# Three column tiles (32, 32 and 64 wide) in place of two of 64 in the expert products of a transformer block

## What is computed

```python
hg = jnp.einsum('nd,edf->nef', tk, we_gate).astype(jnp.float32)
hu = jnp.einsum('nd,edf->nef', tk, we_up).astype(jnp.float32)
act = (jax.nn.silu(hg) * hu * gk[..., None]).astype(tk.dtype)
return jnp.einsum('nef,efd->nd', act, we_down).astype(jnp.float32)
```

## Time and profile before

| what | value |
|---|---|
| median of 2 runs | 1309.55 us (1309.27 to 1309.84) |
| span of the profiled execution | 1309.2 us |
| its own time | not listed apart; the two runs lie 0.1 and 0.6 us above its span |
| expert loop (first to last matmul of L1188) | 632.5 to 1247.0 us |
| PE busy | 1257.5 us, 96% |
| mean granted TensorE clock | 0.986 of full speed |

### The profile page before, as it was taken

The page is one execution under the profiler, slowest core; times in us unless marked ns, Lnnn a source line. Parts: engine busy times, 40 slices in busy tenths (PEclk is TensorE's granted clock), DMA queues, the critical chain, the costliest instruction groups (busy, mean ns, idle before and its releaser), DMA issues.

```text
span 1309.2 us, 22611 instructions
## 1 busy us (share of the span) xinstructions
PE 1257.5 (96%) x6217; PEld 714.6 (55%) x6217; DVE 837.3 (64%) x1769; ACT 737.0 (56%) x964; POOL 191.5 (15%) x373
## 2 busy tenths in 40 slices
PE   2999999999999999989999999999999999999996
PEld 2778788876777788875433333333333333333332
DVE  6746778567787655797556555555565555555578
ACT  3356462334544422212477777777777777777711
POOL 1000000000100100131122222122212221222100
PEclk9799999998999999998999999999999999999999
DMA  8722446659843370545779999999999999998395
GB/s 322 245 65 96 154 138 223 225 188 231 224 162 66 118 268 33 185 163 207 276 309 376 344 401 407 388 383 407 403 352 406 381 404 392 397 403 331 108 389 235
DMA packets 111458, 353.67 MB, mean 270 GB/s; under 512 B 20502, under 2 KB 59527, under 8 KB 85810
## 3 DMA queue, kind: packets, MB, share of 16 engines
q1 hardware_dynamic: 92498, 303.05, 62.5%
q0 software_dynamic: 18912, 50.01, 10.5%
HBM read 326.08 MB, written 47.21 MB: 285 GB/s over the span
## 4 chain that ended last, share of the span: by engine, by line
PE 83%; DVE 11%; DMA 2%; issue 2%; ACT 1%; POOL 0%; SPq 0%; DVEq 0%; ACTq 0%; POOLq 0%
PE bank L1188 27%; PE bank L1213 13%; PE bank L882 10%; PE bank L884 9%; PE bank L883 9%; PE bank L1175 4%; PE bank L1198 2%; PE bank L951 2%; PE bank L1077 2%; PE bank L975 1%; DVE acc_first L1653 1%; DMA y_all<-y_rows 1%; DVE x L2310 1%; PE bank L962 1%; DMA x_rows<-u_rows,row_index 1%
## 5 line engine op out<-in xcount | busy, mean ns | idle before, releaser
L1188 PE MATMUL bank<-gu_use,x_t 128*64 128x512 f32 x1664 | 368.5, 595 | 0.0
L1526 ACT ACTIVATE gu_use<-gu 128x1024 f32 x208 | 209.0, 1058 | 51.8 <-PE bank L1188 36.5
L1188 PEld LDWEIGHTS bank<-gu_use,x_t 128*64 128x64 f32 x1664 | 114.9, 137 | 216.4 <-issue 216.2
L1519 ACT ACTIVATE down_use<-down 128x2048 f32 x103 | 190.9, 1900 | 0.0
L1213 PE MATMUL bank<-down_use,act_t 128*64 128x512 f32 x832 | 187.4, 592 | 0.0
L882 PE MATMUL bank<-h_hi,w_lo 128*128 128x512 f32 x448 | 182.9, 408 | 2.3 <-DVE w_lo L1670 1.3
L884 PE MATMUL bank<-h_hi,w_hi 128*128 128x512 f32 x448 | 176.7, 394 | 0.0
L883 PE MATMUL bank<-h_lo,w_hi 128*128 128x512 f32 x448 | 176.6, 394 | 0.0
L2184 DVE COPY gu_use<-gu 128x1024 f32 x208 | 133.0, 690 | 53.7 <-PE bank L1188 33.3
L1670 DVE TENSOR_TENSOR w_lo<-stream,w_hi 128x1024 fp32r<-128x1024 f32 x72 | 87.9, 1221 | 98.3 <-ACT w_hi L1303 98.2
L2150 DVE TENSOR_TENSOR pick<-slot_id,places 128x512 bf16<-128x512 f32 x53 | 36.7, 692 | 145.5 <-POOL columns L797 145.5
(11 more groups left out here) (323 smaller groups left out, 1664.7 us busy)
## 6 DMA issues: line engine op xcount, KB each, us to landing
gu<-in_we_gate SPq DMA_DIRECT2D x64, 1024.0 KB
gu<-in_we_up SPq DMA_DIRECT2D x64, 1024.0 KB, 8.8
down<-in_we_down SPq DMA_DIRECT2D x64, 1024.0 KB, 8.7
stream<-in_w_in SPq DMA_DIRECT2D x28, 1024.0 KB, 7.1
ada_w<-in_w_ada POOLq DMA_DIRECT2D x8, 2048.0 KB, 9.7
y_rows<-zeros SPq DMA_DIRECT2D x8, 2048.0 KB, 14.7
y_all<-y_rows SPq DMA_DIRECT2D x8, 2048.0 KB, 14.9
ada_first<-in_w_ada SPq DMA_DIRECT2D x16, 512.0 KB, 10.4
```

The lines of the kernel that those rows point to most:

```text
L1188: last = nc.tensor.matmul(bank[item.par][rows, :], x_t[:, k, rows], gu_use[h][:, :, k, :], start=(k == 0), stop=(k == KD - 1))
L1519: nc.scalar.activation(down_use[h][:, :, :], down[:, bass.ds(slot, 1), :, :].rearrange("p o k n -> p (o k) n"), ACT.Copy).then_inc(down_ta ...
L1526: return nc.scalar.activation(gu_use[h][:, 1, ks, :], gu[:, bass.ds(slot, 1), 1, ks, :].rearrange("p o k n -> p (o k) n"), ACT.Copy)
```

## The change

`BY_COLUMNS` names three column tiles: slots 0 to 31 and 32 to 63, both with the weights of half 0, and slots 64 to 127 with those of half 1. Both products loop over these three in place of the two halves. What is computed, the operands in memory, the PSUM banks, the semaphores and their counts are as before. For each block there are three matmuls in place of two, two of them 32 columns wide, and these two stream the same moving operand.

```diff
 HP = P // 2
+BY_COLUMNS = ((0, slice(0, HP // 2)), (0, slice(HP // 2, HP)), (1, slice(HP, P)))
 MIN_PAIRS = T * TOPK // (4 * HP)
...
                     for k in range(part * KD // 2, (part + 1) * KD // 2):
-                        for h in range(2):
-                            rows = slice(h * HP, (h + 1) * HP)
+                        for h, rows in BY_COLUMNS:
                             last = nc.tensor.matmul(bank[item.par][rows, :], x_t[:, k, rows], gu_use[h][:, :, k, :],
                                                     start=(k == 0), stop=(k == KD - 1))
                     last.then_inc(gu_half, 1)
...
                     for f in range(FE):
-                        for h in range(2):
-                            rows = slice(h * HP, (h + 1) * HP)
+                        for h, rows in BY_COLUMNS:
                             last = nc.tensor.matmul(bank[5 + half][rows, :], act_t[:, f, rows], down_use[h][:, f, cols],
                                                     start=(f == 0), stop=(f == FE - 1))
                 last.then_inc(y_done, 1)
```

## The result

| what | before | after |
|---|---|---|
| median of 2 runs | 1309.55 us | 2002.1 us (2001.81 to 2002.39) |
| ratio, 95% interval | | 1.5281 (1.5248 to 1.5313) |
| span of the profiled execution | 1309.2 us | 2000.1 us |
| mean granted clock | 0.986 | 0.994 |

The forecast was 2000 us. The kernel is slower by half, and all of the loss is in the expert loop. In the changed kernel the lines before `gate_up` lie one further down, the down product is L1212, and the code behind it one line up.

The account below looks back on a forecast made before the run. TensorE was taken to bound the expert loop: 10.30 us of streaming and 2.98 us of shape changes, 13.28 us an item, times 52 = 690 us on 1309.2 us, giving 2000 us; range 1845 to 2204 us.

Parts of the forecast that it names:

- TensorE sets the end of the loop: Expert loop, 11.90 us an item: whatever is added to TensorE's stream is added to the time, 52 times.
- A change of the tile's shape empties the array, whether or not the columns meet: Each block of both products: narrow tiles stream, array empties, 64-wide tile streams alone, array empties again; serial case 0.80.
- Rival (a): Blocks of L1188 and L1213: all three tiles stream together, no added streaming, 1310 us; chance 0.14.
- rival (b): Blocks of both products: two streams at a time, third tile waits without emptying, 268 us more, 1577 us; chance 0.03.
- Streaming: 12 x 0.858 us an item: Twelve blocks an item in gate_up and project_down: 1.716 us each in place of 0.858, adding 10.30 us an item.
- The changes: 0.14 into 64 and 0.12 into 32: Changes of tile width, twelve each way an item, less one 0.14 already there: 2.98 us an item.
- The rest of the kernel stays: Outside TensorE's added loop time: what lies beside it costs nothing, and all before 632 us is unchanged.
- Rival (c): Loop: serial case with granted clock falling to 1.2 GHz, every streaming pass doubles, about 3070 us; chance 0.03.

Follow-up runs that it names:

- Experiment 4: Changed kernel with only two tiles, 32 columns at 0 and 64 at 64, slots 32 to 63 left out: 1997.04 us; kernel before 1311.67 us.
- experiment 1: Changed kernel with four tiles of 32 columns in both products: 1312.83 us, ratio 0.9997 to the kernel before.
- experiment 6: Changed kernel with three tiles of 32 columns at 0, 32 and 64, slots 96 to 127 left out: 1309.13 us; kernel before 1310.79 us.
- experiment 5: Changed kernel with two tiles, 48 columns at 0 and 64 at 64, slots 48 to 63 left out: 1309.98 us; kernel before 1310.79 us.
- Experiment 3: Changed kernel with the same 32, 32 and 64 tiles grouped by width, 8 width changes an item, not 24: 1892.28 us, ratio 1.441 to the kernel before.
- experiment 2: Changed kernel with even blocks as two tiles of 64, odd blocks as four of 32: 1390.66 us, ratio 1.059 to the kernel before.
- experiment 7: Changed kernel with 32, 32 and 64 in gate and up only, down product in two tiles of 64: 1768.54 us, ratio 1.347 to the kernel before.

## Why the prediction was right

- *TensorE sets the end of the loop.* Right: the loss is TensorE's own terms, item by item, while DVE and ACT did the same work as before and the DMA engines fell to 0.46 of their time. Whether DMA, at 0.93 before, would have held the loop if TensorE had been any faster was not tried.
- *A change of the tile's shape empties the array, whether or not the columns meet.* This was the step on which everything hung, and the rows of before could not decide it: in each of them the new tile covered columns in use, and a rule by which only such a tile waits would have given the same gaps. The prediction said so and chose, at 0.80; that the choice held is in part luck. Experiment 4 shows it for columns that never meet, experiments 1 and 6 that neither the number of tiles nor the shared operand matters, and experiment 5 sharpens it: the class counts, not the number of columns. Rival (a), three together, falls by the result itself, and rival (b), two at a time, by experiments 1, 4 and 6. "Emptying" is the name for what the rows show: nothing of the other class is loaded or started until the streaming has ended and 0.10 us more have passed. What goes on in the array meanwhile no row shows.
- *Streaming: 12 x 0.858 us an item.* Right. Experiment 3 takes most changes of width away and leaves this term nearly alone: an item of it is 11.22 us over the 11.90 of before, where 10.30 of streaming and 0.89 of changes were expected.
- *The changes: 0.14 into 64 and 0.12 into 32.* Slightly small. Twelve blocks of 1.985 in place of 0.858 are 13.5 us, less the change of 0.14 that stood before gate_up already: 13.37 us an item measured (25.27 less 11.90), 13.28 forecast. What was left out is the stagger of the second narrow tile, 0.007 a block, which is hidden while the width stays and open at each change (experiments 2 and 4 fit this). It is 12 x 0.007 x 52 = 4.4 us.
- *The rest of the kernel stays.* Nearly. It came out shorter, which hid most of the loop's excess: luck, if of 0.2% only. From the first gate_up to the end of the last down product the profiled executions took 1951.32 - 630.72 = 1320.6 us against 1258.37 - 632.54 = 625.8: 694.8 us more, where 690 were forecast. The stretch before the loop was 1.8 us shorter in this execution, and the tail 2.0 us shorter (2000.1 - 1951.32 against 1309.2 - 1258.37). The span grew 690.9 us in sum. No experiment was made on this, but the two traces show where it lies. Ahead of the loop, the lower clock level fell on other stretches. From 296 to 303 us the kernel before was granted 0.51 of the clock, and the same matmuls (L883 at 297.33 to L951 at 303.23) took it 5.90 us; the kernel after, at 1.00 there, took 3.28 us for them (L884 at 298.24 to L952 at 301.52). Other such stretches give part of these 2.6 us back. In the tail, PE of the kernel before waited 0.99 us for a DMA (the first line below), with the DMA engines at 1.00 of their time from 1258 to 1270 us; in the kernel after they were at 0.45 in that place (1951 to 1963), and PE's timeline has no such wait (the second line). The rest of the 2.0 us stays open. So does why the median after, 2002.1, lies 2.0 us above the span of its profiled execution, where the prediction added 0.35; that is the larger part of what the forecast of 2000 missed.

```profile
1276.79 5.42 PE L1265 MATMUL bank<-y_all,ident 128*128 128x512 f32 x12 [0.99 <-DMA y_all<-y_rows]
...
1968.59 5.31 PE L1264 MATMUL bank<-y_all,ident 128*128 128x512 f32 x12
```

- *The clock.* Rival (c) didn't happen: with half of the columns idle at any time through 1303 us the granted clock was 1.00, the level of 2.4 GHz.

## What to carry to other kernels

In these runs column tiles shared the array only with tiles of their own class; one narrow tile in a stream of wide ones costs the time of both and some 0.13 us at each change, though no column is used twice. So make all tiles of a stream one class, even if that means more matmuls (four of 32 cost no more than two of 64) or unused columns (48 in a tile of 64), and where classes must mix, group them. Read the packing from the distance between starts and from which records start together; PE was busy for 99.8% of the loop or more in every one of these kernels.

## What the runs showed of the hardware that was not expected

- Four column tiles with four moving streams of 512 float32 columns, two and two the same, run in the time of two tiles: 0.43 us a step, ratio 0.9997. Twice as many matmul instructions had no cost of their own.
- The open load after a change grows with the columns: 0.10 us for 128 and 0.05 for 64, 0.03 for 32 (experiment 1).
- The stagger of 0.007 us between tiles that start together is free in a stream of one class and, as experiments 2 and 4 fit, paid at each change: 1.58 us an item measured in experiment 2, where prices without it gave 1.41.
- A tile can run a full record (0.47 us) ahead of its neighbour into the next product (experiment 7).
